# Other SBUF padding: activations at several offsets modulo 512 bytes from the weights, instead of one

## What is computed

```python
def first_block(x, ...):
    for l in range(2):
        x = x + 0.5 * swiglu_ffn(rmsnorm(x, ffn1_norm[l]), ffn1_w_up[l], ffn1_w_down[l])   # d_ff 2816
        x = x + mixer(rmsnorm(x, mix_norm[l]), ...)      # dilated attention, depthwise conv of 31 taps, gates
        x = x + 0.5 * swiglu_ffn(rmsnorm(x, ffn2_norm[l]), ffn2_w_up[l], ffn2_w_down[l])
        x = rmsnorm(x, final_norm[l])
    return x

def second_block(x, ...):
    for l in range(2):
        p = rmsnorm_2(x, norm1[l]) @ w_in[l]             # u, q, k, v
        x = x + concat(norm(fourier_mix(u)), norm(windowed_gqa(q, k, v))) @ w_o[l]
        up = dwconv_centred(rmsnorm_2(x, norm2[l]) @ w_up[l], conv_w[l], conv_b[l])
        x = x + (silu(gate) * val) @ w_down[l]
    return x
```

## Time and profile before

| | us |
|---|---|
| runs of the kernel before | 1941.79, 1949.97, 1951.9 |
| their median | 1949.97 |
| the profiled execution | 1942.61 |
| its span, first to last instruction | 1940.8 |

### The profile page before, as it was taken

How to read it: one execution, slowest core, us unless ns; L and a number is a source line. 1 busy time by engine, 2 the same in 40 slices (tenths; PEclk the granted TensorE clock), 3 DMA queues, 4 the chain that set the end, 5 groups by cost and what they waited for, 6 DMA issues and landing times.

```text
span 1940.8 us, 38922 instructions
## 1 busy us (share of the span) xinstructions
PE 1896.1 (98%) x15852; PEld 1826.1 (94%) x15852; DVE 1466.7 (76%) x2148; ACT 1105.9 (57%) x1415; POOL 41.8 (2%) x52
## 2 busy tenths in 40 slices
PE   8999999999999999999999999999999999999998
PEld 7999899799999999999988999999889999889998
DVE  6656799887766686578999786656878778779777
ACT  5444666676544464446676765445566556566554
POOL 0000011000000000000100000000000000000000
PEclk9999999999999999999999999999999999999999
DMA  6557699634665555557986256555335554435553
GB/s 245 195 195 259 207 283 264 183 88 147 226 214 191 177 174 201 190 204 242 280 254 170 86 169 221 200 192 174 128 129 189 191 191 159 162 111 198 177 188 141
DMA packets 63308, 368.59 MB, mean 190 GB/s; under 512 B 8416, under 2 KB 8928, under 8 KB 26464
## 3 DMA queue, kind: packets, MB, share of 16 engines
q1 hardware_dynamic: 56144, 341.88, 50.7%
q0 software_dynamic: 6912, 25.17, 7.2%
q10 hardware_dynamic: 144, 0.00, 0.0%
HBM read 359.68 MB, written 1.05 MB: 186 GB/s over the span
## 4 chain that ended last, share of the span: by engine, by line
PE 73%; DVE 16%; ACT 4%; DMA 4%; issue 1%; SPq 0%; DVEq 0%; ACTq 0%
PE bank L460 23%; PE bank L461 22%; PE bank L462 22%; DVE lo L1672 6%; DVE cv L1925 4%; ACT hi L1092 2%; DMA raw<-in_w 2%; DVE zt L1888 1%; DMA zt<-zt 1%; DMA lo<-in_w 1%; PE bank L642 1%; PE bank L669 1%; PE bank L655 1%; PE bank L627 1%; ACT n_hi L1155 1%
## 5 line engine op out<-in xcount | busy, mean ns | idle before, releaser
L1672 DVE TENSOR_TENSOR lo<-raw,hi 128x2048 fp32r<-128x2048 f32 (+1 forms) x336 | 663.6, 1977 | 193.6 <-ACT hi L1092 193.0
L1092 ACT ACTIVATE hi<-raw 128x2048 fp32r<-128x2048 f32 (+1 forms) x336 | 598.7, 1785 | 98.2 <-PE bank L462 79.1
L460 PE MATMUL bank<-n_hi,hi 128*128 128x256 f32 x2256 | 633.7, 281 | 17.3 <-DVE lo L1952 7.8
L461 PE MATMUL bank<-n_lo,hi 128*128 128x256 f32 x2256 | 626.9, 278 | 0.0
L462 PE MATMUL bank<-n_hi,lo 128*128 128x256 f32 x2256 | 626.8, 278 | 0.0
L460 PEld LDWEIGHTS bank<-n_hi,hi 128*128 128x128 f32 x2256 | 426.9, 189 | 23.5 <-DVE lo L1952 7.8
L461 PEld LDWEIGHTS bank<-n_lo,hi 128*128 128x128 f32 x2256 | 425.6, 189 | 1.3 <-issue 1.0
L462 PEld LDWEIGHTS bank<-n_hi,lo 128*128 128x128 f32 x2256 | 425.3, 189 | 0.0
L460 PE MATMUL bank<-h_hi,hi 128*128 128x256 f32 x1152 | 330.3, 287 | 8.5 <-DVE h_lo L1676 4.3
L461 PE MATMUL bank<-h_lo,hi 128*128 128x256 f32 x1152 | 320.8, 279 | 0.0
L462 PE MATMUL bank<-h_hi,lo 128*128 128x256 f32 x1152 | 320.8, 278 | 0.0
(11 more groups left out here) (273 smaller groups left out, 2324.8 us busy)
## 6 DMA issues: line engine op xcount, KB each, us to landing
raw<-in_w SPq DMA_DIRECT2D x286, 1024.0 KB, 4.9
raw<-in_w SPq DMA_DIRECT2D x53, 512.0 KB, 3.8
lo<-in_w POOLq DMA_DIRECT2D x48, 512.0 KB, 9.0
zt<-zt SPq DMA_DIRECT2D x96, 64.0 KB, 6.6
bv<-in_bv SPq DMA_DIRECT2D x2, 768.0 KB, 6.2
spread<-in_spread SPq DMA_DIRECT2D x2, 768.0 KB, 9.0
x<-in_x SPq DMA_DIRECT2D x4, 256.0 KB, 5.7
out_x<-sq SPq DMA_DIRECT2D x1, 1024.0 KB, 3.9
```

The costliest lines, as they stand in the source:

```text
L460: mm(out, w_hi, a_hi, start=start, stop=False, skip_group_check=True)
L461: mm(out, w_hi, a_lo, start=False, stop=False, skip_group_check=True)
L1092: fn(hi[:, s, 0:w], raw[:, s, 0:w], ACT.Copy).then_inc(sem["hi"], 1)
L1672: v.tensor_tensor(lo[:, s, 0:w], raw[:, s, 0:w], hi[:, s, 0:w].bitcast(F32), ALU.subtract)\
```

## The change

```diff
@@ build @@
     lo = sb("lo", [P, SLOTS, CW], F32R)
-    state["at"] += 192
     x = sb("x", [P, KT, S], F32)
     h_hi = sb("h_hi", [P, KT, S], F32R)
     h_lo = sb("h_lo", [P, KT, S], F32R)
@@
+    state["at"] += 384
     at_a = state["at"]
     qk = sb("qk", [P, 24, S], F32)
     s_hi = sb("s_hi", [P, KT, S], F32R, at_a)
     s_lo = sb("s_lo", [P, KT, S], F32R, at_a + KT * S * 4)
+    state["at"] += 256
     at_v = state["at"]
     v_sb = sb("v", [P, 2, GROUPS * 512], F32)
     hid_hi = sb("hid_hi", [P, 2, S], F32R, at_v)
@@
     psq = sb("psq", [P, KT, S], F32, at_a)
+    state["at"] += 448
     at_u = state["at"]
     upad = sb("upad", [P, KT, UPW], F32)
     n_hi = sb("n_hi", [P, KT, S], F32R, at_u)
```

## The result

The changed kernel takes 1981.65 us (median of four runs, 1979.31 to 1983.32); the kernel before 1948.02 in the same comparison. The ratio is 1.019, with a 95% interval of 1.016 to 1.022. It is slower by some 34 us. The forecast, 1947 us and no measurable change, was wrong, and the time lies just above its range, 1922 to 1980.

The account below looks back on a forecast made before the run. TensorE's matmul spacing was taken as the bound. The profiled 1942.6 us, plus zero for the new offsets and 0 to 9 us for redrawn levels, gave a median of 1947 us, range 1922 to 1980.

Parts of the forecast that it names:

- the two levels, 4.45 ns apart: Gaps between successive 256-column `mm3` matmuls on TensorE: 113.3 ns fast, 117.8 ns slow, each level lasting between breaks.
- the last sentence of the prediction: Wrong if a tensor takes its level by its offset in all streams; each group then moves by its own price.
- zero for the relation's own effect: In `mm3` streams, the new offsets from the weights were taken to add 0 us, within +47.4 to -13.8 us.
- The slow rival: New offsets make `mm3` streams enter the slow level after every break; 1963 to 1990 us if `n` is hit; chance 0.25.
- About all of it on the path: Nearly all of the `mm3` gap changes, +47.4 to -13.8 us, would show in the time, because TensorE is the path.
- The prices: Cost per `mm3` group if all its gaps turned slow: `n` 23.2 us, `h` 9.8, `hid` 10.4, small groups 4.0.
- The third level, near 109 ns,: Rival: `mm3` gaps fall below 113.3 ns, to 108.9 ns, giving 1867 us or part of it; chance 0.06.
- The spread of before: Unchanged kernel's runs, 1941.79 to 1951.9 us: the 7.4 us from profiled run to median read as more slow `mm3` gaps.

Follow-up runs that it names:

- the shifted one: Weights and activations all moved 64 bytes higher together, against the kernel before, their distance still 192; 1946.5 us, ratio 0.999.

## Why the prediction was wrong

- **What bounds the kernel and the two levels, 4.45 ns apart,** held. TensorE's spacing is what counted, other engines' instructions did not move, and the groups moved one by one, as the last sentence of the prediction said they would if it was wrong.
- **The step that failed first** is the inference from the earlier trace rows: the same loop on the same addresses runs at either level, so the address can't be all that picks it. That is true at 192, but it says nothing of other offsets, and the forecast used it as if a new offset only meant a new draw with the same odds. At 64 the same two levels came out with other odds (98 gaps of 100 on `n` slow, where 22 of 100 had been), and 0, 96, 128, 160 and 224 have gaps of their own above both. I had seen one offset and took its behaviour for that of all.
- **The term that failed with it, zero for the relation's own effect,** measured 55.9 us in the gaps and 34 us in the time. It rested on the weights streaming with 320 as their relation: 229 ns, nearer to twice the fast level than to twice the slow. Different lengths of stream were compared as if the gap went with the columns, and the relation was of another kind (weights slot streaming, activation loaded). With an activation streaming, `n` at 320 has 117.6 ns. The row was also the low one of three: over all starts of the trace of before, the 512-column gaps are 229.4 ns with `h`, 231.1 with `n` and 235.0 with `f` stationary, all at the same relation. And what is good for one kind isn't for the other: with `h` at 0 these gaps fell to 227.8 ns in the changed kernel, while the gaps in which `h` streams became the longest. No row bore on the question.
- **The slow rival** had the right mechanism for `n`, one that enters the slow level at nearly every start: 22.5 us measured in the gaps, 23.2 foretold for all slow, and the 142 gaps that stayed fast are 0.6 us. It was too cheap for `h` and `hid`, for it let no gap go over 117.8 ns. `h` went to 119.9 (16.3 us, not 9.8) and `hid` to 118.6 (12.7 us, not 10.4). The top of the range, 1980, left out nearly all streams slow as unlikely; that case came in.
- **"About all of it on the path"** was wrong the other way: 19.8 of 58.6 us went into waits that had been there, the largest part of them in the stretches on `h`. Without this the changed kernel would have taken about 2000 us.
- **A slip in the working:** `n` has 6646 gaps, 5205 fast and 1441 slow, not 6746. The prices were worked out from the two parts and stand.
- **The rule of the Trainium skill** ("TensorE: Matmul & The Clock Gate", "Step-by-step: what each phase is for") that the weights' load and the running matmul have read ports of their own and don't take from one another was read as saying that all offsets are alike. With these float32r streams the offsets differ by up to 6.6 ns in 113.3, and moving only the weights' `lo` half is enough to bring every group to 117.5 ns or more. Whether it is the load of the next weights that meets the running matmul, which is what the rule denies, is not shown; the 127.4 ns on `h` with `lo` apart speaks for it.
- **The third level, near 109 ns,** was not met at any of the eight offsets; the shortest gaps of the main streams are 112 ns.
- **The spread of before** seems to have been read rightly: the median run itself has no profile, but the second profile at the unchanged distance, of 1950.0 us, is 7.4 us longer and has 5.4 of these in its gaps (1585.0 against 1579.6 us), with two FFNs slow instead of one.

Still open: what in the chip meets what. The distance modulo 256 bytes is shown to matter, and moving the weights' `lo` half alone shows that it is the distance to the weights; that the load of the next weights is the partner, and not the matmul's own, is only hinted at by the 127.4 ns in the one run with `lo` apart. What decides, after a break, which of the two levels a stream at 192 or 64 enters is open too.

## What to carry to other kernels

Where TensorE is the bound and every matmul loads new weights, measure the gap from start to start by group; the length of the records, 276 against 281 ns, hides what the starts show. In a stream of float32r matmuls of 256 columns the distance between streamed operand and weights modulo 256 bytes was worth up to 6% of the gap and 1.9% of this kernel, so fix it, give all streams the same good one, and look at each offset on one group at a time: one kernel can carry four or five. And when a trace has only one value of what a change varies, it can't price the change; widen the range to both sides instead of taking zero.

## What the runs showed of the hardware

Gaps of `mm3` matmuls at full clock depend on the distance to the weights modulo 256 bytes: 113.3 ns at best (192), 119.9 at worst (0, 96). At 192 there are two levels, 113.3 and 117.8 ns. In the profiles of the kernel before and of the shifted one, each holds for a whole stream without a break, through `n`, `hid` and `last` of an FFN, over 1500 gaps at most. At 64 and 320 there are the same two, but only stretches of up to 94 gaps (in the profiles of four kernels) had the fast one. At 0, 32, 96, 128, 160 and 224 no stretch of 12 gaps ran at it. What VectorE and ScalarE did made little difference: in the changed kernel `h`'s mean gap was 119.8 ns over the 1784 gaps that began with both busy, and 120.0 over the 167 that began with both idle, from the starts in its trace.
